# Attention through ready products of weights and memory, six weight slots, and a gate tile in two passes

## The chip, the cores and the metric

The kernel runs on one core of a Trainium2 chip. The metric is device time in microseconds (us), from the start of the program to its end; lower is better. Four compute engines work beside each other: TensorE (PE), VectorE (DVE), ScalarE (ACT) and GpSimd (POOL). SyncE (SP) issues most of the transfers, POOL and ACT issue some. The engines wait for one another by semaphores.

## The reference, cut to what matters

One layer of a hybrid decoder: 2048 prompt tokens and 8 decode tokens, model width 1024, 256 memory tokens, 4 attention heads of 256, a feed-forward width of 2816, all in fp32. The mixer before the attention (four heads of a gated short convolution and an mLSTM in chunks, then `w_out`) takes gates from a projection of 8 columns, 4 input and 4 forget gates.

```python
def mem_kv(mem, g_mem, w_xkv):
    kk, vv = jnp.split(rmsnorm(mem, g_mem) @ w_xkv, 2, axis=-1)
...
def cross_attn(xn, mk, mv, w_xq, w_xo):
    q = (xn @ w_xq).reshape(B, T, X_HEADS, X_HEAD_DIM)
    s = jnp.einsum('bthd,bmhd->bhtm', q, mk) * (X_HEAD_DIM ** -0.5)
    p = jax.nn.softmax(s, axis=-1)
    o = jnp.einsum('bhtm,bmhd->bthd', p, mv).reshape(B, T, X_HEADS * X_HEAD_DIM)
    return o @ w_xo
...
    hp = hp + mp
    hp = hp + cross_attn(rmsnorm(hp, g_cross[l]), pk, pv, w_xq[l], w_xo[l])
    hs = hs + cross_attn(rmsnorm(hs, g_cross[l]), cache_mem_k[l], cache_mem_v[l], w_xq[l], w_xo[l])
    hp = hp + swiglu(rmsnorm(hp, g_ffn[l]), w_gu[l], w_down[l])
```

The prompt attends to keys and values (`pk`, `pv`) made from 256 memory tokens; each of the 8 decode tokens has its own cached ones.

## The kernel before, in words

**Layout.** Activations stand feature-major: 8 tiles of 128 features on the partitions, tokens as columns. The prompt is cut into five blocks of 4, 3, 3, 3 and 3 chunks of 128 tokens (`BLK`). The decode tokens ride along as 8 more columns: in block `DM` for the mixer, in block `DO` for `w_out` and the queries, in block `DX` for the output projection and the feed-forward part.

**The stream of weight tiles.** All projections go through `gemm(g, ...)`. A group `g` is one tile of 128 output features: for each of 8 feature tiles three fp32r matmuls (high weights by high activations, high by low, low by high; together they stand for fp32), 24 in all, into one of three PSUM banks `gb` (L503). Groups 0 to 15 make K and V of the memory; then each block has 121 groups: the gate tile, 4 SIG tiles, 24 for the four mixer heads, 8 OUT, 8 XQ, 8 XO, then the feed-forward ones. While block 0 runs, SP loads each raw tile (512 KB, two slots `w_raw`), ACT makes its high part (`w_high`, L812), POOL its low part (L407), and SP stores the pair (1 MB) to `split_d`; blocks 1 to 4 load the pairs from there into `NS` slots `w_hl`. A slot is free when its group's matmuls are done. For groups 0 to 15 DVE makes the low parts (L1164). In the same opening loop ACT and DVE normalise block 0's input (L1153 scale, L829 high part, L1159 low part).

**Hooks.** Small matmuls are put between those of a weight tile: `hooks={k: f}` runs `f` after feature tile `k`. PE runs in program order, so a hook whose inputs are late stops the weight tiles behind it.

**Gate tile.** Its 24 matmuls give rows for input and forget gates, at partitions 32 apart. `pick_f` is one fp32 matmul in the first SIG tile that brings the forget rows to the partitions of the input rows (L550). `turn_mem` turns V in block 0 (L537).

**Attention.** The XQ tiles give the queries, which DVE and ACT split into high and low parts. `scores(h)` multiplies them with K, 256 columns a matmul (L671); `maxima` (L1422, L1425), `exps` (L1000) and `normalise` (L1431, L1433) make the softmax for one head at a time; `ptrans(h)` turns it by fp32 transposes (L681); `pv(h)` multiplies with V in plain fp32 (L688); `out_high` and `out_low` (L1012, L1438) split the result for the XO tiles. These hooks stand inside the XQ tiles for heads 0 and 1 and between parts of the first three XO tiles for heads 2 and 3. `sumsq` (L511) sums squares for the norms; `turn_row` (L561) turns gate rows into columns.

## Time and profile before

| | us |
|---|---|
| median of 3 timed runs | 2981.76 (2981.4 to 2985.2) |
| the profiled execution's own time | 2983.26 |
| its span in the trace | 2981.4 |
| PE busy | 2932.7 |
| DVE busy | 1212.0 |
| ACT busy | 762.6 |
| POOL busy | 378.2 |

The span is the time from the first to the last recorded instruction; the execution's own time has some microseconds around it. Busy times of different engines overlap. Busy PE time contains the time in which a matmul ran at a lowered clock.

### The profile page before, as it was taken

How to read it: one execution, taken by the hardware profiler on the slowest of the kernel's cores; microseconds unless marked ns; L12 is line 12 of the kernel's file. 1: busy time of each engine (PE TensorE's matmuls, PEld its weight loads, DVE VectorE, ACT ScalarE, POOL GpSimd, SP SyncE). 2: the span in 40 equal slices, each digit the busy share in tenths (PEclk: the TensorE clock that was granted, in tenths of full speed). 3: DMA queues.
4: the chain of work that ended last, by engine and by line, in shares of the span. 5: the costliest groups of instructions: out<-in, count | busy, mean ns of one | idle time of the engine just before them, and what ended most of it. 6: DMA issues, size and time to landing. Idle time of an engine off the chain costs nothing.

```text
span 2981.4 us, 39316 instructions
## 1 busy us (share of the span) xinstructions
PE 2932.7 (98%) x16212; PEld 2771.1 (93%) x16212; DVE 1212.0 (41%) x2327; ACT 762.6 (26%) x1510; POOL 378.2 (13%) x251
## 2 busy tenths in 40 slices
PE   7999999999999999999999999999999999999998
PEld 7778778888899999999999999999999999999998
DVE  6355554234624344233344546334322243442223
ACT  4433433232332220113232011322311032231001
POOL 0443434444210000000000111000000000000000
PEclk9999999999999999999999999999999999999999
DMA  5876858789776498777667989866467777647775
GB/s 198 318 261 221 281 199 302 267 283 317 283 279 245 159 328 301 267 265 282 216 227 269 339 323 370 304 225 251 170 242 260 261 258 274 227 176 250 254 268 193
DMA packets 126873, 776.11 MB, mean 260 GB/s; under 512 B 15172, under 2 KB 18692, under 8 KB 46952
## 3 DMA queue, kind: packets, MB, share of 16 engines
q1 hardware_dynamic: 109840, 710.78, 65.7%
q0 software_dynamic: 13904, 59.48, 5.9%
q10 hardware_dynamic: 2952, 3.34, 0.4%
q8 instruction: 130, 2.13, 0.3%
q14 instruction: 47, 0.39, 0.0%
HBM read 633.59 MB, written 139.95 MB: 259 GB/s over the span
## 4 chain that ended last, share of the span: by engine, by line
PE 89%; DMA 4%; DVE 2%; ACT 2%; POOL 1%; issue 1%; SPq 0%; ACTq 0%; DVEq 0%
PE gb L503 82%; DMA w_raw<-w_st 2%; PE ta L671 2%; POOL w_hl L407 1%; DMA w_hl<-split_d 1%; PE tb L688 1%; PE td L688 1%; ACT w_hl L812 1%; DMA w_raw<-w_kv 1%; PE ta L592 0%; DVE w_hl L1164 0%; PE ta L511 0%; PE tb L561 0%; PE gm L681 0%; PE tb L603 0%
## 5 line engine op out<-in xcount | busy, mean ns | idle before, releaser
L503 PE MATMUL gb<-xn_hi,w_hl 128*128 128x384 f32 (+2 forms) x6480 | 1795.7, 351 | 10.7 <-DVE xn_lo L1159 4.3
L503 PEld LDWEIGHTS gb<-xn_hi,w_hl 128*128 128x128 f32 x6480 | 1188.5, 188 | 70.8 <-DMA w_hl<-split_d 5.8
L503 PE MATMUL gb<-xn_lo,w_hl 128*128 128x384 f32 (+2 forms) x3240 | 1124.3, 347 | 0.0
L503 PE MATMUL gb<-act_hi,w_hl 128*128 128x384 f32 (+3 forms) x3296 | 874.3, 344 | 17.3 <-DVE w_hl L1164 10.7
L503 PEld LDWEIGHTS gb<-act_hi,w_hl 128*128 128x128 f32 x3296 | 599.3, 189 | 44.9 <-DVE w_hl L1164 11.0
L503 PEld LDWEIGHTS gb<-xn_lo,w_hl 128*128 128x128 f32 x3240 | 610.4, 188 | 29.0 <-issue 1.4
L503 PE MATMUL gb<-act_lo,w_hl 128*128 128x384 f32 (+3 forms) x1648 | 564.1, 342 | 0.0
L1207 DVE TENSOR_TENSOR work<-gb,r_res 128x384 f32<-128x384 f32 (+2 forms) x260 | 151.7, 585 | 633.4 <-PE gb L503 570.4
L407 POOL TENSOR_TENSOR w_hl<-w_raw,w_hl 128x1024 fp32r<-128x1024 f32 x121 | 294.6, 2439 | 484.8 <-ACT w_hl L812 484.8
L503 PEld LDWEIGHTS gb<-act_lo,w_hl 128*128 128x128 f32 x1648 | 311.9, 189 | 13.4 <-issue 0.7
L1393 DVE TENSOR_TENSOR x<-x,gb 128x384 f32<-128x384 f32 (+2 forms) x200 | 115.3, 581 | 374.6 <-PE gb L503 371.9
L812 ACT ACTIVATE w_hl<-w_raw 128x1024 fp32r<-128x1024 f32 x132 | 138.9, 1057 | 323.5 <-DMA w_raw<-w_st 160.4
L1069 ACT ACTIVATE work<-work 128x384 f32<-128x384 f32 (+2 forms) x110 | 59.9, 545 | 504.6 <-DVE work L1207 504.5
L1072 ACT ACTIVATE act_hi<-work 128x384 fp32r<-128x384 f32 (+2 forms) x110 | 60.0, 546 | 345.5 <-DVE work L1620 345.5
L986 ACT ACTIVATE work<-x 128x384 f32<-128x384 f32 (+2 forms) x120 | 65.5, 546 | 270.1 <-DVE x L1393 249.8
L1403 DVE TENSOR_TENSOR r_res<-r_res,work 128x384 f32<-128x384 f32 (+2 forms) x120 | 94.6, 788 | 69.2 <-ACT work L986 67.7
L1620 DVE TENSOR_TENSOR work<-work 128x384 f32<-128x384 f32 (+2 forms) x110 | 86.6, 787 | 30.7 <-ACT work L1069 20.5
L876 ACT ACTIVATE big<-gb,cst 128x384 f32<-128x384 f32 (+1 forms) x80 | 48.6, 608 | 197.0 <-PE gb L503 196.8
L378 POOL DMA_DIRECT2D big<-rows_d x20 | 10.9, 550 | 684.4 <-DMA rows_d<-big 684.4
L1607 DVE TENSOR_TENSOR act_lo<-work,act_hi 128x384 fp32r<-128x384 f32 (+2 forms) x110 | 85.6, 778 | 14.5 <-ACT act_hi L1072 13.9
L1303 DVE TENSOR_TENSOR work<-ta,big 128x128 f32<-128x128 f32 x64 | 18.6, 291 | 150.4 <-ACT work L957 150.4
L1406 DVE SCALAR_TENSOR_TENSOR xn_lo<-x,cst,xn_hi 128x384 fp32r<-128x384 f32 (+2 forms) x80 | 55.8, 697 | 0.0
(246 smaller groups left out, 1809.0 us busy)
## 6 DMA issues: line engine op xcount, KB each, us to landing
w_hl<-split_d SPq DMA_DIRECT2D x484, 1024.0 KB, 5.1
split_d<-w_hl SPq DMA_DIRECT2D x121, 1024.0 KB, 5.0
w_raw<-w_st SPq DMA_DIRECT2D x121, 512.0 KB, 5.9
w_raw<-w_kv SPq DMA_DIRECT2D x16, 512.0 KB, 3.4
big<-kd_d POOLq DMA_DIRECT2D x8, 1024.0 KB, 8.4
big<-vd_d POOLq DMA_DIRECT2D x8, 1024.0 KB, 11.4
x<-x_blk POOLq DMA_DIRECT2D x8, 768.0 KB, 8.9
big<-x_blk POOLq DMA_DIRECT2D x6, 768.0 KB, 6.1
```

Source lines behind the costliest of these rows:

```text
L407: pool.tensor_tensor(w_lo[:, g % NS, :], w_raw[:, g % NR, :], w_hi[:, g % NS, :].bitcast(F32), ALU.subtract).then_inc(w_lo_done, 1)
L503: mm = pe.matmul(gb[:, ps, 0:wd], a[:, s, k * P:(k + 1) * P], r[:, k, 0:wd], start=(first and k == ks[0] and i == 0), stop=(last and k == ...
L671: mm = pe.matmul(ta[:, t // 2, (t % 2) * 256:(t % 2) * 256 + 256], a[:, kt, t * P:(t + 1) * P], r[:, kt, :], start=(dt == 0 and i == 0), s ...
L812: act.activation(w_hi[:, n % NS, :], w_raw[:, n % NR, :], ACT.Copy).then_inc(w_hi_done, 1)
L986: act.activation(sq_res[:, 0:wd], x[:, e, 0:wd], ACT.Square).then_inc(res_sq, 1)
L1069: act.activation(et[:, 0:W], gt[:, 0:W], ACT.Silu).then_inc(e_ffn, 1)
L1072: act.activation(act_hi[:, f, 0:W], ht[:, 0:W], ACT.Copy).then_inc(hid_hi, 1)
L1207: return lambda ps: v.tensor_tensor(dst[:, 0:wd], ps[:, 0:wd], r_res[:, 0:wd], ALU.mult)
L1393: return lambda ps: v.tensor_tensor(x[:, e, 0:wd], x[:, e, 0:wd], ps[:, 0:wd], ALU.add)
L1403: v.tensor_tensor(acc_res[:, 0:wd], acc_res[:, 0:wd], sq_res[:, 0:wd], ALU.add).then_inc(res_acc, 1)
L1607: v.tensor_tensor(act_lo[:, f, 0:W], ht[:, 0:W], act_hi[:, f, 0:W].bitcast(F32), ALU.subtract).then_inc(hid_lo, 1)
L1620: v.tensor_tensor(ht[:, 0:W], et[:, 0:W], ut[:, 0:W], ALU.mult).then_inc(h_ffn, 1)
```

## The change

**Products.** A new phase stands between the K/V groups and block 0's gate tile. For the keys it multiplies `w_xq` of a head with that head's K, for the values that head's V with `w_xo`: 32 banks of 128x512, 12 matmuls of 256 columns each for the 16 banks of keys, 6 of 512 for the 16 of values. ACT copies the high part of a bank into one of four slots `made`, DVE subtracts the low part, and ACT issues two stores of 256 KB to where the XQ and XO pairs of `split_d` stand, in runs of 1 KB (keys) or 512 B (values). The 16 raw tiles that this takes (`w_xq` transposed, `w_xo`) come through `w_raw`, ACT and POOL ahead of block 0. Block 0 then loads its XQ and XO tiles from `split_d`, as the others do. `next_scale`, `next_high` and `next_low` for block 0 stand in this phase.

**Attention in a block.** `wide(p)` makes the scores of two heads at a time: 128 tokens stand still, the product moves, 512 columns a matmul, 24 per chunk and pair. The RMS norm comes in as a factor by token inside the softmax; `sum_cols` makes it with one-column matmuls and `norm_cols` on ACT. The turned softmax goes directly, in high and low parts (`prob_high`, `prob_low`), through XO tiles that hold V times `w_xo`. Separate scores, `pv` and `turn_mem` are gone.

**Gate tile.** Its columns 64 to 127 are the low parts of the weights (POOL copies them into the high tile), so two passes do. ACT copies the bank out, DVE adds the rows of the low columns and shifts the forget rows; the row work runs on 32 partitions (`ROWS`), and `pick_f` is gone.

**Decode tokens.** Their queries and attention outputs no longer ride along. `decode_queries` (in XO tiles 3 to 6 of block `DO`) and `decode_outputs` (in OUT tiles 3 to 6 of block `DX`) make them with 8 rows against raw weight rows, 32 fp32 matmuls of 512 columns in all, from four slots `dwt` that POOL loads in 16 transfers of 512 KB; `turn_outputs` turns the result with 8 small matmuls. More pieces of the decode attention stand at other tiles (`PIECE_AT`).

**The rest.** `NS` goes from 5 to 6. Two pairs of mixer hooks in each head are merged into one.

```diff
+G_MEM = 16
+G_KV = 32
+NPRE = 32
...
-NS = 5
+NS = 6
...
+        made = big[:, 4096:8192].rearrange("p (i s c) -> p i s c", i=4, s=2)
...
+                    pool.tensor_tensor(lo_w, raw_w, hi_w.bitcast(F32), ALU.subtract).then_inc(gate_low, 1)
+                    pool.wait_ge(gate_low, 1)
+                    lo_part, hi_part = (w.rearrange("p (k c) -> p k c", k=KT)[:, :, 64:P] for w in (lo_w, hi_w))
+                    pool.tensor_copy(hi_part, lo_part.bitcast(F32)).then_inc(w_lo_done, 1)
...
+            def decode_rows(i):
+                after(pool, dw_used, i - 3)
+                pool.dma_start(dwt[:, i % 4, :], w_dec[i] if i < KT else w_kv[G_MEM + i]).then_inc(dw_loaded[i % 4], 16)
...
+                passes = [(w_hi, hi), (w_hi, lo), (w_lo, hi)]
+                if g >= G_KV and (g - G_KV) % G_BLK == O_GATE:
+                    passes = passes[0:2]
...
+            def pre_bank(i):
+                if i < NP:
+                    read_out(pe, G_MEM - NP + i)
+                else:
+                    pe.wait_ge(pre_lo, i - NP + 1)
+                return gb[:, (G_MEM + i) % NP, :]
+            for h in range(HEADS):
+                pe.wait_ge(mem_lo, 2 * h + 2)
+                for j in range(4):
+                    i = h * 4 + j
+                    bank = pre_bank(i)
+                    for n in range(2):
+                        for dt in range(2):
+                            g = G_MEM + 2 * h + dt
+                            if j == 0 and n == 0:
+                                slot_ready(g)
+                            c = (2 * j + n) * P
+                            for f, (a, r) in enumerate([(w_hi, act_hi), (w_hi, act_lo), (w_lo, act_hi)]):
+                                mm = pe.matmul(bank[:, n * NMEM:(n + 1) * NMEM], a[:, g % NS, c:c + P], r[:, 2 * h + dt, NMEM:2 * NMEM],
+                                               start=(dt == 0 and f == 0), stop=(dt == 1 and f == 2))
+                    if j < 3:
+                        mm.then_inc(pre_done, 1)
+                    else:
+                        mm.then_inc(group_done, 2)
+            for h in range(HEADS):
...
+                for j in range(4):
+                    i = HEADS * 4 + h * 4 + j
+                    bank = pre_bank(i)
+                    mt, half = j // 2, j % 2
+                    for dt in range(2):
+                        g = G_MEM + KT + 2 * h + dt
+                        if j == 0:
+                            slot_ready(g)
+                        for f, (a, r) in enumerate([(act_hi, w_hi), (act_lo, w_hi), (act_hi, w_lo)]):
...
-                def pick_f():
-                    read_out(pe, gw(b, O_GATE))
-                    pe.matmul(td[:, 0:w_mix(b)], pick, gi[:, 0:w_mix(b)], start=True, stop=True).then_inc(f_picked, 1)
...
+                    c_hooks = {2: lambda: t_part(h, 0), 6: lambda: t_part(h, 1) or n_part(h, 0)}
                     if CH == 3:
-                        c_hooks = {2: lambda: t_part(h, 0), 4: lambda: t_part(h, 1), 7: lambda: n_part(h, 0)}
-                        h_hooks = {1: lambda: t_part(h, 2), 3: lambda: n_part(h, 1), 7: lambda: n_part(h, 2)}
...
-                def scores(h):
-                    pe.wait_ge(q_lo_done, b * 8 + 2 * h + 2)
-                    if h == 0:
-                        pe.wait_ge(r_done, r_res_at(b, 0))
-                    after(pe, exp_done, ch0(b, h))
+                def sum_cols():
+                    pe.wait_ge(res_acc, b * 27 + 9)
                     for t in range(CH):
-                        for dt in range(2):
-                            kt = 2 * h + dt
-                            for i, (a, r) in enumerate([(act_hi, mem_k_hi), (act_lo, mem_k_hi), (act_hi, mem_k_lo)]):
-                                mm = pe.matmul(ta[:, t // 2, (t % 2) * 256:(t % 2) * 256 + 256], a[:, kt, t * P:(t + 1) * P],
-                                               r[:, kt, :], start=(dt == 0 and i == 0), stop=(dt == 1 and i == 2))
-                        if t % 2 or t == CH - 1:
-                            mm.then_inc(s_done, 1)
-                def ptrans(h):
-                    pe.wait_ge(p_done, ch0(b, h) + CH)
-                    after(pe, o_lo, b * 8 + 2 * h)
-                    for mt, bank in enumerate((gm, tb)):
+                        mm = pe.matmul(td[:, t:t + 1], acc_res[:, t * P:(t + 1) * P], ones[:, 0:1], start=True, stop=True)
+                    if b == DO:
+                        mm = pe.matmul(td[0:NDEC, CHM:CHM + 1], acc_res[:, DC:DC + NDEC], ones[:, 0:1], start=True, stop=True)
+                    mm.then_inc(ssq_done, 1)
+                def score_bank(p, t):
+                    if p == 0:
+                        return gb[:, (gw(b, O_XQ) + t) % NP, :] if t < NP else gm[:, :]
+                    return (ta[:, 0, :], ta[:, 1, :], td[:, :], tb[:, :])[t]
+                def ptrans(h, mt):
+                    bank = gm if b == 0 and h < 2 else (gm, tb)[mt]
+                    pe.wait_ge(p_done, ch0(b, h // 2 * 2 + 2))
+                    pe.wait_ge(o_lo, b * 8 + 2 * h + mt - 1) if b or h == 3 else after(pe, o_lo, 2 * h + mt * (h < 2))
+                    for t in range(CH):
+                        m = pe.transpose(bank[:, t * P:(t + 1) * P], prob[:, t, h % 2, mt * P:(mt + 1) * P], ident)
+                    m.then_inc(pt_done, 1)
...
+                def wide(p, hooks):
+                    for q in range(4):
+                        g = gw(b, O_XQ) + 4 * p + q
+                        slot_ready(g)
                         for t in range(CH):
-                            m = pe.transpose(bank[:, t * P:(t + 1) * P], prob[:, t, mt * P:(mt + 1) * P], ident)
-                        m.then_inc(pt_done, 1)
-                def pv(h):
-                    pe.wait_ge(pt_evac, (b * HEADS + h) * 2 + 2)
-                    for dt, bank in enumerate((td, tb)):
-                        for mt in range(MT):
-                            mm = pe.matmul(bank[:, 0:TOK], mem_v[:, mt, h * 256 + dt * P:h * 256 + (dt + 1) * P],
-                                           prob_t[:, mt, 0:TOK], start=(mt == 0), stop=(mt == MT - 1))
-                        mm.then_inc(pv_done, 1)
-                opening(gw(b, O_XQ), W, 0)
-                q_hooks = {3: {3: lambda: scores(0)}, 4: {6: lambda: ptrans(0)}, 5: {1: lambda: scores(1), 4: lambda: pv(0)},
-                           6: {4: lambda: ptrans(1), 7: lambda: scores(2)}, 7: {3: lambda: pv(1)}}
-                for m in range(2, KT):
-                    gemm(gw(b, O_XQ + m), W, xn_hi, xn_lo, hooks=q_hooks.get(m))
+                            if q == 0 and p == 0 and t < NP:
+                                read_out(pe, gw(b, O_OUT + KT - NP) + t)
+                            if q == 0 and p == 1 and t == 2:
+                                pe.wait_ge(rcol_done, b + 1)
+                            for n in range(2):
+                                kt = 2 * q + n
+                                if p == 0 and t == 0:
+                                    pe.wait_ge(res_lo, b * 16 + kt + 1)
+                                for f, (a, r) in enumerate([(xn_hi, w_hi), (xn_lo, w_hi), (xn_hi, w_lo)]):
+                                    mm = pe.matmul(score_bank(p, t), a[:, kt, t * P:(t + 1) * P], r[:, g % NS, n * 512:n * 512 + 512],
+                                                   start=(kt == 0 and f == 0), stop=(kt == KT - 1 and f == 2))
+                            if t == CH - 1:
+                                mm.then_inc(group_done, 1)
+                            elif q == 3:
+                                mm.then_inc(s_done, 1)
+                            if (q, t) in hooks:
+                                hooks[q, t]()
+                wide(0, {(1, CH - 1): sum_cols})
+                if b == 0:
+                    wide(1, {(1, 3): lambda: ptrans(0, 0), (2, 1): lambda: ptrans(0, 1), (2, 3): lambda: ptrans(1, 0),
+                             (3, 1): lambda: ptrans(1, 1)})
+                else:
+                    wide(1, {(1, 2): lambda: ptrans(0, 0) or ptrans(0, 1), (2, 2): lambda: ptrans(1, 0) or ptrans(1, 1)})
...
                 xo(0, 0)
-                ptrans(2)
                 xo(1, 0)
-                scores(3)
                 xo(2, 0)
-                pv(2)
                 xo(0, 1)
+                ptrans(2, 0)
+                ptrans(2, 1)
                 xo(1, 1)
-                ptrans(3)
-                xo(0, 2)
-                xo(1, 2)
-                pv(3)
                 xo(2, 1)
-                xo(2, 2)
-                for i in range(3):
-                    xo(i, 3)
+                ptrans(3, 0)
+                ptrans(3, 1)
+                for h in (2, 3):
+                    for i in range(3):
...
+            def store_made(i):
+                act.wait_ge(pre_lo, i + 1)
+                h, j = (i // 4) % HEADS, i % 4
+                for s in range(2):
+                    if i < NPRE // 2:
+                        dst = split_d[O_XQ + 4 * (h // 2) + j, :, s, :].rearrange("p (n h m) -> p n h m", n=2, h=2)[:, :, h % 2, :]
+                        act.dma_start(dst, made[:, i % 4, s, :].rearrange("p (n m) -> p n m", n=2)).then_inc(pre_stored[i % 4], 16)
+                    else:
+                        kt, m0 = 2 * h + j // 2, O_XO + j % 2 * 4
+                        dst = split_d[m0:m0 + 4, :, s, kt * P:(kt + 1) * P].rearrange("m p c -> p m c")
+                        act.dma_start(dst, made[:, i % 4, s, :].rearrange("p (m c) -> p m c", m=4)).then_inc(pre_stored[i % 4], 16)
+            for i in range(NPRE):
+                pre_made(act, i)
+                after(act, pre_stored[i % 4], 32 * (i // 4))
+                act.activation(made[:, i % 4, 0, :].bitcast(F32R), gb[:, (G_MEM + i) % NP, :], ACT.Copy).then_inc(pre_hi, 1)
+                if i:
+                    store_made(i - 1)
+                if i % 4 == 3:
+                    w_high(G_MEM + i // 4 * 2)
+                    w_high(G_MEM + i // 4 * 2 + 1)
+                if i < KT:
+                    read_out(act, G_MEM - 1)
+                    act.activation(act_hi[:, i, 0:NMEM], vfeat[:, i, :], ACT.Copy).then_inc(mem_hi, 1)
...
+                def prob_high(h):
+                    for mt in range(MT):
+                        act.wait_ge(pt_done, pt0 + 2 * h + mt + 1)
+                        bank = gm if b == 0 and h < 2 else (gm, tb)[mt]
+                        act.activation(act_hi[:, 2 * h + mt, 0:TOK], bank[:, 0:TOK], ACT.Copy).then_inc(o_hi, 1)
...
+                v.wait_ge(gates_out, b + 1)
+                v.tensor_tensor(fg[:, 0:W], gb[96:96 + ROWS, g % NP, 0:W], gates[32:32 + ROWS, 0:W], ALU.add).then_inc(f_ready, 1)
+                v.tensor_tensor(gi[:, 0:W], gb[64:64 + ROWS, g % NP, 0:W], gi[:, 0:W], ALU.add).then_inc(out_v, 1)
```

## Rows read from the trace of the kernel before

**Rows 1.** The page: busy time and share of the span; chain by engine.
```profile
PE 2932.7 (98%) x16212; PEld 2771.1 (93%) x16212; DVE 1212.0 (41%) x2327; ACT 762.6 (26%) x1510; POOL 378.2 (13%) x251
PE 89%; DMA 4%; DVE 2%; ACT 2%; POOL 1%; issue 1%; SPq 0%; ACTq 0%; DVEq 0%
```

**Rows 2.** Windows: stretch, us, then busy us by engine, clock, DMA share, GB/s.
```profile
0.00:71.50 71.50, 54.22 (x388) 51.41 (x388) 47.40 (x73) 36.67 (x55) 5.39 (x6) 0.95 0.58 195
71.50:92.00 20.50, 14.34 (x42) 10.62 (x41) 14.48 (x19) 7.82 (x13) 8.74 (x5) 0.75 0.91 321
...
650.00:2981.40 2331.40, 2314.08 (x13245) 2258.18 (x13243) 891.34 (x1876) 509.55 (x1100) 139.64 (x144) 1.00 0.72 260
```

**Rows 3.** Chain of waits in block 4: start us, us, engine, tile, line, instructions.
```profile
2565.40 5.22 PE gb L503 x30
...
2618.46 2.15 PE ta L671 x18
...
2632.27 1.29 PE td L688 x4
```

**Rows 4.** Chain of waits in block 0.
```profile
92.00 0.86 PE td L550 x2
...
94.24 0.44 PE ta L537 x4
94.68 5.47 PE gb L503 x24
...
353.43 2.87 PE ta L671 x24
```

**Rows 5.** Chain of waits, gate rows turned in a later block.
```profile
2454.01 0.56 PE tb L561 x6
```

**Rows 6.** Waits of PE: who was waited for, us in total, times, longest.
```profile
PE gb L503 <- DMA w_hl<-split_d: 2.9, 6, 0.7
PE gm L681 <- DVE work L1433: 2.4, 5, 0.5
PE ta L671 <- DVE act_lo L1448: 1.7, 1, 1.7
```

**Rows 7.** DMA queues (packets, MB, share) and issues (KB each, us to landing).
```profile
q1 hardware_dynamic: 109840, 710.78, 65.7%
...
q10 hardware_dynamic: 2952, 3.34, 0.4%
...
w_raw<-w_kv SPq DMA_DIRECT2D x16, 512.0 KB, 3.4
...
big<-x_blk ACTq DMA_DIRECT2D x1, 2048.0 KB, 12.3
...
dec<-st_conv ACTq DMA_DIRECT2D x1, 32.0 KB, 1.8
```

**Rows 8.** Timeline and operations of ACT, DVE and POOL in the front.
```profile
0.76 2.21 ACTq L796 DMA_DIRECT2D x<-mem_x  x4
...
75.27 1.06 ACT L812 ACTIVATE w_hl<-w_raw 128x1024 fp32r<-128x1024 f32 x1 [4.36 <-DMA w_raw<-w_st]
...
66.13 0.69 DVE L1159 TENSOR_TENSOR xn_lo<-big,xn_hi 128x512 fp32r<-128x512 f32 x1
...
69.55 2.89 DVE L1159 TENSOR_TENSOR xn_lo<-big,xn_hi 128x512 fp32r<-128x512 f32 x1
...
76.41 2.40 POOL L407 TENSOR_TENSOR w_hl<-w_raw,w_hl 128x1024 fp32r<-128x1024 f32 x1 [4.51 <-ACT w_hl L812]
```

**Rows 9.** Groups by shape, ACT and DVE in the attention: busy, mean ns, idle before.
```profile
L1012 ACT ACTIVATE act_hi<-tb 128x512 fp32r<-128x512 f32 x4 | 2.4, 600 | 4.5 <-PE tb L688 4.5
...
L1000 ACT ACTIVATE work<-ta,work 128x256 f32<-128x256 f32 x64 | 29.6, 471 | 48.7 <-DVE work L1425 48.7
...
L1422 DVE TENSOR_REDUCE work<-ta 128x2 f32<-128x512 f32 x24 | 16.6, 690 | 24.9 <-PE ta L671 24.9
...
L1433 DVE TENSOR_SCALAR work<-work 128x256 f32<-128x256 f32 x64 | 22.6, 354 | 2.3
```

More of the change, by code:

```diff
@@ L520, in _ @@
             sumsq(acc_mix, td, NMEM)
-            for g in range(2, G_KV):
+            for g in range(2, G_MEM):
                 gemm(g, NMEM, act_hi, act_lo)
@@ L848, in _ @@
             act.wait_ge(x0_loaded, 16)
-            for g in range(G_KV):
+            for g in range(G_MEM):
                 if g < 4:
@@ L1020, in _ @@
-                rnorm(r_res, ta[:, 0, :], r_res_at(b, 0), W)
-                for m in range(2):
-                    w_high(gw(b, O_XQ + m))
-                q_high(0)
-                q_high(1)
-                q_high(2)
+                    if b == DX and e == KT - 2:
+                        act.wait_ge(dw_used, 2 * KT)
+                        for half, bank in enumerate((ta[:, 1, :], td)):
+                            act.activation(dwt[0:NDEC, 0, half * 512:half * 512 + 512], bank[0:NDEC, :], ACT.Copy).then_inc(qrow_done, 1)
@@ new lines, in _, with exps @@
+                pt0 = b * 8
+                def exps(p):
+                    after(act, pt_done, pt0 + 4 * p)
+                    for t in range(CH):
+                        act.wait_ge(mx_done, ch0(b, 2 * p) // 2 + t + 1)
+                        bank = score_bank(p, t)
+                        for i in range(2):
+                            act.activation(prob[:, t, i, :], bank[:, i * NMEM:(i + 1) * NMEM], ACT.Exp, scale=r_sc[:, t:t + 1],
+                                           bias=mx[:, t, i, 1:2], accum_out=mx[:, t, i, 2:3]).then_inc(exp_done, 1)
@@ L1176, in _ @@
             v.wait_ge(x0_loaded, 16)
-            for g in range(G_KV):
+            for g in range(G_MEM):
                 dst = mem_k if g < KT else vfeat
@@ L1472, in _ @@
+                for p in range(2):
+                    maxima(p, 0)
+                    for t in range(1, CH):
+                        maxima(p, t)
+                        normalise(p, t - 1)
+                    normalise(p, CH - 1)
+                    prob_low(2 * p)
+                    prob_low(2 * p + 1)
                 if b == DM:
@@ L1711 @@
         st += [chunk(wi, o + h * P) for s, o in enumerate(order) if s != 3]
[L1712 to L1713 removed]
+    st += [chunk(np.asarray(w_out)[0], m * P) for m in range(KT)]
+    st += [np.zeros((P, D), f) for _ in range(2 * KT)]
     gu, dn = np.asarray(w_gu)[0], np.asarray(w_down)[0]
```

528 lines of the change are left out of this document (292 added, 236 removed).

## The prediction

> **What bounds the kernel now.** I read the page's busy times first: TensorE (PE) is busy 98% of the span and holds 89% of the chain that ended last [rows 1]. The windows then say where that is not so: from 650 us on PE is busy 2314 of 2331 us at full clock, but in the first 71.5 us it is busy 54, and around the first gate tile 14 of 20.5 at a mean granted clock of 0.75, part of it at 1.2 GHz and part at 2.4 [rows 2]. So from about 92 us on, a PE microsecond taken away or added is a microsecond of the end; before that, the front of the kernel is set by loads and by ScalarE (ACT), VectorE (DVE) and GpSimd (POOL). The change does both: it removes PE work late and puts a new phase of small work at the front. The chain of waits prices each PE instruction at full rate, and I use those pieces.
>
> PE's prices: 24 fp32r matmuls 512 wide take 5.47 us, .228 each [rows 4]; 30 that are 384 wide 5.22, .174 each [rows 3]. A score stretch is 18 matmuls in 2.15 us, 24 in block 0 in 2.87, so .120 for 256 columns [rows 3, 4]. A plain fp32 matmul is two instructions: 512 wide .86 [rows 4], 384 wide .645 (1.29 for two) [rows 3], one of 4 columns .187 (0.56 for three) [rows 5].
>
> **Removed, all on PE's path.** The separate scores: 4 heads in 4 blocks of three chunks and in block 0, 16x2.15 + 4x2.87 = 45.9. The products with V in fp32: per head four of 384 or 512 columns, 16x2.58 + 4x3.44 = 55.0. Turning V (turn_mem): 4x.44 = 1.8 [rows 4]. The pick matmul: .86 + 4x.65 = 3.5. The gate tile's third pass in blocks 1 to 4: 8 matmuls x .174 x 4 = 5.6 (block 0's is in the front, below). The XQ tiles become the scores: before, 192 matmuls per block, 384 wide in three blocks, 392 in one, 512 in block 0 (33.4, 34.0 and 43.8 us); after, xn stands still and the product moves, 48 matmuls of 512 per chunk: 144x.228 = 32.8 with three chunks, 192 with four. That is .6x3 + 1.2 = 3.0 less. XO without the decode columns: 192 matmuls x 8 columns, .7. Sum 115.5.
>
> **Added to the same path.** The decode tokens' queries and outputs are now fp32 products of 8 rows against 512 moving columns: 16 tiles x 2 halves x .86 = 27.5. This is where the change pays for its saving: 8 columns riding along cost next to nothing. The small turns add 8x.19 = 1.5. sum_cols is 17 one-column fp32 matmuls, at most 17x.19 = 3.2, in place of sums that cost .86 + 4x.65 = 3.5, so -.3. Sum +28.7. Decode rows come by POOL's queue as 16 tiles of 512 KB, beside a queue that is 66% busy [rows 7]; nothing of the decode tokens' softmax is more urgent than before. The merged hooks of the mixer carry the same work; I cost them at nothing, and their cover is the weight matmuls queued on both sides (one hook that arrives late would cost what `work` now costs in such places, under 1 us each).
>
> **The new front.** Now the gate's pick matmul stands at 92.0, after 15 matmuls of the first SIG tile, so that tile would begin at 88.4 at full clock. After the change the weight phase for K and V ends about where it does now, 71 us, because its DVE work is less while one more tile comes through. Then 32 banks of products follow before the gate. For one bank PE needs 12x.120 = 1.44 us (K side) or 6x.228 = 1.37 (V side). ACT copies 512 columns out, .60 [rows 9], issues two DMAs, .55 each (four took 2.21) [rows 8], and makes a hi half of a raw tile every second bank, .53 a bank; with the K, V or xn copy of .4 to .6 on each of the first 16 banks that is 2.8 us. DVE subtracts, .69 [rows 8], and has scale and low of another tile in the first half; when POOL works beside it, such an operation took 2.89 instead of .69 [rows 8]. DMA stores 512 KB a bank in runs of 1 KB or 512 B: the small-packet queue of ACT moved 3.34 MB in 0.4% of the span, which is 280 GB/s or 1.87 us for 512 KB, and half a raw tile at q1's rate (710.78 MB in 65.7%, 363 GB/s) is .72 more [rows 7].
>
> So ACT sets the first 16 banks, 16x2.8 = 45 us. For the last 16 ACT has 1.7 + .53 = 2.2 and DMA 1.87 + .72 = 2.6, less when the raw tiles are all in; with two kept 1 MB block-0 tiles going out beside them I take 40. Start: the pairs of raw tiles must pass ACT and POOL (3.4 + 1.06 + 2.40 us for load, hi and lo) [rows 7, 8], so the chain of banks begins near 75. The gate then begins at 75 + 45 + 40 = 160, takes 16x.228 = 3.6, and some 2 us for a clock that has fallen as it had here, 0.75 [rows 2]; SIG begins at 165.6 instead of 88.4: **+77**.
>
> A page of the Trainium skill, "DMA: Bandwidth & Descriptors", section Bandwidth, says a DMA costs about 2.0 us plus its bytes at 436 GB/s and wants at least 1 MiB in one. By it a 256 KB store would take 2.6 us when alone, 5.2 for a bank whose two do not overlap; the rows agree on the fixed part only in that 512 KB land in 3.4 us [rows 7]. The same page, section Bandwidth, part "Why small descriptors are slow", speaks against runs of 256 B and not of the 512 B that are used here; no row tells the two apart.
>
> Of the waits, those of scores on q's low part (1.7) and on weight slots that arrive late (2.9) [rows 6] mostly go with the scores and the sixth slot: -4. Sum: 2983.3 + 77 - 115.5 + 28.7 - 4 = 2969.5. The profiled execution took 1.5 us more than the median run, so **2968**.
>
> **The softmax cover**, which I cost at nothing: the last chunk of the second pair goes through maximum .69, two exps .47 each, and two normalisations .35 each [rows 9], 2.3 us; with the reciprocal, the column operations and the handovers I take 3.5. Until the turns PE has 24 matmuls of XO, 24x.174 = 4.2 us (5.5 in block 0). Without that cover the chain would cost its 3.5 in five blocks, 17.
>
> **Bounds.** Front: PE alone would make it 32x1.44 = 46 us and not 85. At the other end, the 2 MB ACT load landed in 12.3 us [rows 7], 170 GB/s, 3.1 us for a bank's stores, with .72 then 3.8 a bank, 122 in all. I take 85 because ACT's own row is nearest; both ends go into the range. sum_cols: 0 to 3.2. Waits: 0 to -8. Hooks: 0 to +5. Break-even: slower by 0.2% needs the front to take 19 us longer, (85+19)/32 = 3.25 us a bank.
>
> **Rivals.**
> (a) The front keeps pace with PE, stores and copies hidden behind it: 46 instead of 85, 2929. For it: ACT's and DVE's copies alternate over three banks. Against: ACT's own work is already 2.8 a bank by its rows. Chance .07.
> (b) The other side, slower than before: the stores land slowly, so that each of the four `made` slots comes free late and ACT waits for it in order, with hi parts and DVE queued behind. At 3.8 us a bank the front is 122, +37: 3005. It decides from 3.25 us a bank. For it: 170 GB/s on ACT's load [rows 7], the small pieces of the stores, and DMA engines that are 91% busy at 321 GB/s around the gate already [rows 2]. Against: 280 GB/s for this queue's small packets. Chance .19.
> (c) The softmax takes the place of the removed waits: today PE waits for normalise five times, 2.4 us in all [rows 6]. If DVE falls one chunk (.69 + .71 [rows 9] and, as an estimate, .45 for its small column operations: 1.85) further behind, five blocks cost 9: 2978. Chance .11.
> (d) The ACT queue's stores run one after another with a fixed part each. A store of 256 KB then takes .7 of transfer and the 1.8 that 32 KB took to land here [rows 7]: 64x2.5 = 160 instead of 85, +75, 3043. This is the skill's fit told as a mechanism ("DMA: Bandwidth & Descriptors", section Bandwidth); its figure gives 64x2.6 = 166, an estimate. Against: four of ACT's loads of 256 KB were in flight together. Chance .03.
> (e) The change does not do what it says: scores as moving products would need the 101 us to come back elsewhere. PE's instruction counts exclude it; .03 is left for anything unnamed.
>
> **How the numbers follow.** Forecast .57 with its own range 2955 to 2985 (front 72 to 101 us, waits 0 to -8). 0.2% is 6 us (2975.8 to 2987.7), about what a measurement of this kernel can tell. Faster: .46 of the forecast, all of (a), .02 of (c), .02 of the rest, together .57. The same: .11 + .07 of (c) + .02 of (b) = .20. Slower: .17 of (b), .02 of (c), .03 of (d), .01 of the rest, .23. The range 2945 to 3006 leaves out (a), (d) and a tail of (b).
>
> **What would show it.** Right: SIG of block 0 begins at 160 to 170 us; PE's busy time falls by about 40 (removed 115.5, added 28.7, products 45); ACT and not DMA releases the waits between the banks; no PE wait for DVE over 1 us in the ptrans of blocks 1 to 4; a block's attention is about 20 us shorter. Wrong: waits of ACT for stores (b, d), of transposes for normalise (c), or a decode product that waits for its rows. What would make the number wrong is above all the front: each 0.3 us a bank is 10 us.

## The result: 0.4% slower

The changed kernel takes 2994.37 us (median of 7, 2992.7 to 2995.53) against 2981.76 for the kernel before on the same chip: ratio 1.004, 95% interval 1.0029 to 1.0051. The forecast was 2968, faster with .57; what came is on the side of rival (b), slower, at .19 with 3005, but by another mechanism, as the runs below show. The profiled execution has a span of 2991.6 against 2981.4, so +10.2 is what has to be explained, where the sum gave -13.8.

The page after, busy times and the chain by engine:

```profile
PE 2911.8 (97%) x15801; PEld 2721.9 (91%) x15801; DVE 1176.5 (39%) x2259; ACT 745.3 (25%) x1470; POOL 387.3 (13%) x268
PE 87%; DMA 6%; DVE 2%; ACT 2%; POOL 1%; issue 1%; ACTq 0%; SPq 0%; DVEq 0%
```

PE is 21 us less busy than in [rows 1], where the prediction counted on about 42 (115.5 removed, 28.7 and 45 added); the products alone kept PE busy for 53.0 us (25.5 at L642, 27.5 at L660) and not 45, at a mean granted clock of 0.83 in the stretch. The span is 10 us longer: PE waits 31 us more. The windows show where:

```profile
0.00:71.50 71.50, 51.22 (x348) 48.42 (x348) 40.41 (x65) 33.80 (x51) 3.45 (x6) 1.00 0.56 187
71.50:92.00 20.50, 14.64 (x96) 13.59 (x95) 16.77 (x17) 8.30 (x15) 11.08 (x5) 0.84 0.53 176
92.00:129.00 37.00, 26.46 (x159) 24.33 (x158) 27.22 (x33) 20.49 (x35) 16.40 (x7) 0.86 0.85 286
129.00:171.60 42.60, 22.92 (x78) 17.18 (x79) 12.11 (x18) 15.08 (x22) 18.36 (x9) 0.83 1.02 329
171.60:210.00 38.40, 34.12 (x140) 27.77 (x140) 8.28 (x14) 12.56 (x18) 11.90 (x5) 0.90 0.94 343
210.00:220.00 10.00, 10.00 (x30) 7.87 (x31) 1.42 (x2) 6.05 (x5) 7.00 (x6) 0.57 0.76 244
```

The columns are those of [rows 2]. Up to 92 us the DMA engines are about half busy (0.56 and 0.53) and PE waits; from 129 to 171.6 they are full (1.02) and PE is 54% busy; and the loss goes on after the gate tile, to 220 us.

The front in the timeline of ACT (start, us, operation, idle time before it and its releaser): the last high part before the banks, the first bank's copy, two pairs of store issues, and the copy of the gate tile.

```profile
83.95 1.06 ACT L980 ACTIVATE w_hl<-w_raw 128x1024 fp32r<-128x1024 f32 x1 [1.86 <-DMA w_raw<-w_kv]
84.91 0.40 ACT L1046 ACTIVATE act_hi<-x 128x256 fp32r<-128x256 f32 x1
85.22 0.58 ACT L1064 ACTIVATE big<-gb 128x512 fp32r<-128x512 f32 x1
...
100.16 0.89 ACTq L1055 DMA_DIRECT2D split_d<-big  x2
...
154.78 5.60 ACTq L1059 DMA_DIRECT2D split_d<-big  x2
...
178.38 0.69 ACT L1094 ACTIVATE big<-gb,cst 128x512 f32<-128x512 f32 x1 [0.94 <-PE gb L595]
```

The bank loop begins with the first bank's copy by ACT, at 85.2 us (forecast: near 75). The 17th comes at 128.9 and the 32nd at 170.2, so the two halves take 44 and 41 us, where 45 and 40 were forecast. The raw tiles that set the 85.2 are seen in the chain of waits:

```profile
73.08 3.68 DMA w_raw<-w_kv
76.79 1.07 ACT w_hl L980
...
77.92 2.40 POOL w_hl L472
80.33 3.59 DMA w_raw<-w_kv
83.95 1.06 ACT w_hl L980
```

A load, its high part and its low part, 7.2 us for a pair of tiles, because only two raw slots exist: the next raw tile is loaded when the low part has been made. PE does not appear there at all. In the first 16 banks the profile's chain passes twice through the landing of a store, behind which ACT gets a free `made` slot. This is the mechanism of rival (b); it is there, but small beside the 85 us of the banks:

```profile
100.56 4.10 DMA split_d<-big
...
112.10 4.00 DMA split_d<-big
```

PE itself waits in the banks for the low part by DVE (25.9 us in all, at L660 and L642), which follows ACT's copy. The prediction had named ACT as the releaser.

The late part of the kernel is as costed. Block 1's attention in the chain (start, us, tile):

```profile
1047.79 0.56 PE td L803 x6
1048.35 8.31 PE gb L839 x36
1056.66 2.72 PE ta L839 x12
...
1074.33 4.19 PE gb L595 x24
1078.51 0.33 PE gm L821 x3
1078.84 0.33 PE tb L821 x3
1079.17 2.10 PE gb L595 x12
```

Wide scores take .227 to .231 a matmul, sum_cols .56 for three, and the 24 XO matmuls (4.19) hide the softmax, the one wait for it being .8 us in block 0: no wait stands between them and the turns at L821. From block 0's second sum of squares to block 1's the trace has 601.7 us instead of 623.2, 21.5 less.

### The profile page after: what moved, and what is told of

Read it like the earlier page. It is cut to its first block, busy times and chain, and to the rows that moved or that the text cites. A ratio compares the mean times of both kernels' runs of the same rounds, so it can differ in the third digit from the quotient of the medians.

```text
span 2991.6 us, 38477 instructions
## 1 busy us (share of the span) xinstructions
PE 2911.8 (97%) x15801; PEld 2721.9 (91%) x15801; DVE 1176.5 (39%) x2259; ACT 745.3 (25%) x1470; POOL 387.3 (13%) x268
## 4 chain that ended last, share of the span: by engine, by line
PE 87%; DMA 6%; DVE 2%; ACT 2%; POOL 1%; issue 1%; ACTq 0%; SPq 0%; DVEq 0%
PE gb L595 76%; PE gb L839 3%; DMA w_raw<-w_st 2%; PE ta L839 2%; DMA w_raw<-w_kv 2%; POOL w_hl L472 1%; PE td L839 1%; ACT w_hl L980 1%; DMA big<-kd_d 1%; DMA w_hl<-split_d 1%; PE ta L708 0%; PE tb L683 0%; DVE work L1515 0%; DMA split_d<-big 0%; PE gm L821 0%
## 5 line engine op out<-in xcount | busy, mean ns | idle before, releaser
L595 PE MATMUL gb<-xn_hi,w_hl 128*128 128x384 f32 (+2 forms) x5800 | 1588.4, 350 | 6.5 <-issue 4.3
L595 PEld LDWEIGHTS gb<-xn_hi,w_hl 128*128 128x128 f32 x5800 | 1063.0, 188 | 56.0 <-issue 8.1
L595 PE MATMUL gb<-xn_lo,w_hl 128*128 128x384 f32 (+2 forms) x2920 | 1014.0, 347 | 0.0
L595 PEld LDWEIGHTS gb<-xn_lo,w_hl 128*128 128x128 f32 x2920 | 550.3, 188 | 24.6 <-issue 0.5
L1413 DVE TENSOR_TENSOR work<-gb,r_res 128x384 f32<-128x384 f32 (+2 forms) x220 | 128.2, 585 | 549.2 <-PE gb L595 512.3
L1616 DVE TENSOR_TENSOR r_res<-r_res,work 128x384 f32<-128x384 f32 (+2 forms) x120 | 81.4, 679 | 56.5 <-ACT work L1198 54.9
L839 PE MATMUL gb<-w_hl,xn_hi 128*128 128x512 f32 x240 | 77.6, 397 | 0.0
```

Of the source, the lines that this page charges most:

```text
L595: mm = pe.matmul(gb[:, ps, 0:wd], a[:, s, k * P:(k + 1) * P], r[:, k, 0:wd], start=(first and k == ks[0] and i == 0), stop=(last and k == ...
L839: mm = pe.matmul(score_bank(p, t), a[:, kt, t * P:(t + 1) * P], r[:, g % NS, n * 512:n * 512 + 512], start=(kt == 0 and f == 0), stop=(kt ...
L1413: return lambda ps: v.tensor_tensor(dst[:, 0:wd], ps[:, 0:wd], r_res[:, 0:wd], ALU.mult)
L1616: v.tensor_tensor(acc_res[:, 0:wd], acc_res[:, 0:wd], sq_res[:, 0:wd], ALU.add).then_inc(res_acc, 1)
```

## The experiments

Each kernel ran beside the kernel before on the same chip; its median there was 2980.4 to 2981.8 in all. Five times were read from each trace: the first, 17th and 32nd bank copy, the copy of the gate tile, and the second sum of squares of block 0, by which block 0's attention is over.

Each trace is of one execution. e3 and e8 leave out a part of the work and have one run each.

| run | 1st | 17th | 32nd | gate copy | sum | time | ratio (95%) |
|---|---|---|---|---|---|---|---|
| before | | | | 86.5 | 448.3 | 2981.8 | |
| changed | 85.2 | 128.9 | 170.2 | 178.4 | 514.5 | 2994.4 | 1.004 (1.0029 to 1.0051) |
| e1 | 80.2 | 123.7 | 166.3 | 174.3 | 503.6 | 2986.2 | 1.0018 (1.0009 to 1.0027) |
| e2 | 86.4 | 126.5 | 164.6 | 174.8 | 513.5 | 2990.8 | 1.0034 (1.0022 to 1.0047) |
| e3 | 85.3 | 126.4 | 167.2 | 175.9 | 508.2 | 2985.9, one run | |
| e4 | 83.6 | 126.6 | 172.4 | 180.1 | 516.8 | 2992.6 | 1.0043 (1.0028 to 1.0058) |
| e5 | 70.7 | 114.2 | 156.1 | 164.9 | 485.9 | 2967.9 | 0.9954 (0.9939 to 0.9969) |
| e6 | 70.8 | 114.8 | 158.4 | 166.7 | 488.3 | 2969.3 | 0.9958 (0.9941 to 0.9974) |
| e7 | 71.5 | 112.6 | 147.9 | 155.5 | 481.8 | 2963.4 | 0.9940 (0.9925 to 0.9955) |
| e8 | 87.1 | 130.5 | 170.4 | 180.1 | 517.6 | 2982.2, one run | |
| e9 | 70.7 | 110.1 | 144.9 | 151.7 | 473.7 | 2956.4 | 0.9923 (0.9906 to 0.9939) |
| e10 | 70.4 | 111.1 | 146.2 | 153.9 | 475.9 | 2958.0 | 0.9925 (0.9910 to 0.9939) |
| e11 | | | | 80.3 | 432.0 | 2982.4 | 1.0007 (0.9998 to 1.0016) |
| e12 | 83.6 | 127.2 | 170.5 | 177.6 | 513.1 | 2991.4 | 1.0035 (1.0023 to 1.0048) |

### Five slots (e1) and the sixth one later (e12)

```diff
-NS = 6
+NS = 5
```

> The changed kernel with five weight slots. Theory 'the front is late because ACT looks six tiles ahead': ACT enters the bank loop after the high part of one raw tile less, so the first bank copy comes at about 81 us, not 85, and the gate tile begins 3 to 4 us earlier than 171.6; the reload waits of blocks 1 to 4 (2.9 us before) come back; together 2990 to 2995. Rival 'six slots carry the later blocks': the front is unchanged and the waits for split pairs grow past 5 us, over 2998.

The front came as the first theory had it, 5.0 us earlier at the first copy and 4.1 at the gate tile, and the total went lower still, by 8 us (6.7 between the profiled spans). Two things add up. The first is at the very start: in the changed kernel ACT waits in the opening loop for the raw tile of the sixth slot, which lands 7.49 us after it was asked for, with the 2 MB load of x under way, where the tile before took 3.75:

```profile
20.20 0.49 ACT L1023 ACTIVATE act_hi<-x,cst 128x256 fp32r<-128x256 f32 x1
25.50 1.06 ACT L1026 ACTIVATE w_hl<-w_raw 128x1024 fp32r<-128x1024 f32 x1 [4.80 <-DMA w_raw<-w_kv]
```

The first two sums of squares come at 31.3 and 48.3 us with six slots, at 26.7 and 43.3 with five and at 26.0 and 42.5 before. The second is in block 0. Waits of PE from 165 to 460 us with six slots, then with five:

```profile
...
PE gb L595 <- issue: 4.3, 1, 4.3
PE tb L683 <- ACT big L1117: 4.3, 1, 4.3
PE tb L719 <- DVE work L1515: 4.2, 4, 1.2
```

```profile
PE gb L595 <- issue: 6.3, 1, 6.3
PE tb L719 <- DVE work L1515: 5.3, 4, 2.0
...
PE tb L683 <- ACT big L1117: 0.7, 1, 0.7
```

ACT makes the gate rows behind the high parts of tiles six ahead, and those tiles are late; the turn of the rows waits 4.3 us for them with six slots and 0.7 with five. Other waits take part of this back: the wait by `issue` stands before the gate copy, and from that copy to the second sum PE is idle 9.3 us of 336.1 with six slots and 7.0 of 329.3 with five. So 2.3 of the 6.8 us are waiting and 4.5 are busy time. After the long wait in the changed kernel the granted clock is 0.57 for ten us (the window 210 to 220 above, in part at 1.2 GHz), after PE had been busy 5.7 of 10 us; in the same place e1 has 1.00. At 0.57, ten us lose 4.3, nearly all of the 4.5. Against that, from block 0's second sum to the last, six slots take 2466.1 us and five 2470.3: the sixth slot does give back 4 us in the later blocks (with five slots PE waits 3.9 us in all for pairs that are loaded again, with six not at all), and costs 11 up to there.

e12 separates the two. Six slots, the sixth tile's parts made after the normalisation of the memory that the opening loop begins with (ACT's side of the edit; DVE's is the same):

```diff
-                if k < NS:
+                if k < NS - 1:
                     act.wait_ge(w_loaded[k % NR], 16 * (k // NR) + 16)
...
             for g in range(G_MEM):
                 if g < 4:
                     next_sq(0, 2 * g)
+                if g == 0:
+                    act.wait_ge(w_loaded[(NS - 1) % NR], 16 * ((NS - 1) // NR) + 16)
+                    act.activation(w_hi[:, NS - 1, :], w_raw[:, (NS - 1) % NR, :], ACT.Copy).then_inc(w_hi_done, 1)
...
```

> The changed kernel with its six weight slots, but the high and low part of the sixth tile made after the opening normalisation instead of within it. Theory 'the sixth slot costs 5 us at the very start, since ACT and DVE wait in the opening loop for a raw tile that comes behind the 2 MB load of x': the first two sums of squares come at about 26 and 43 us as before (31.3 and 48.3 now), the bank loop still starts late, at 82 to 85 us, since ACT must pass the high part of tile 21 first; total 2989 to 2993. Rival 'the 5 us are made good by the wait for tile 21 anyway': first bank copy at 85, total 2993 to 2996. Rival 'five slots gain because fewer tiles are looked ahead in the bank loop and block 0': the turned gate rows still wait for ACT 4 us.

The first sum is at 27.2 again, but of its 4 us only 1.6 are left at the first bank copy and 0.8 at the gate: the high part of tile 21 has to pass in any case. The other 3.4 us between e12 and e1 (83.6 and 80.2) are one tile of the chain, half of the 7.2. The turned rows still wait 3.6 us. So the opening wait by itself costs little; looking one tile further ahead costs both times, before the banks and in block 0. The total is 2991.4; its interval (1.0023 to 1.0048) overlaps that of the changed kernel (1.0029 to 1.0051), so no gain in time is shown.

### Who sets the banks' pace (e2, e3, e4)

e2 takes ACT's 64 issues away (`store_made` goes to SyncE's queue, four banks at a time between the raw loads).

> The changed kernel with the 64 stores of the product phase issued by SyncE in place of ACT. Theory 'ACT's own work sets the first 16 banks': they fall from 44 us to about 30, the gate tile begins at 155 to 162 instead of 171.6, total 2980 to 2988. Rival 'the phase is bound by bytes that the DMA engines move': the first 16 banks are shorter, the last 16 take as much longer, the gate tile begins at 168 or later, total 2991 or more.

Neither theory: the first half took 40 us, not 30. ACT's issues were 3.5 us of its 43.6; the chain of waits of this run goes through ACT's high parts and then DVE:

```profile
94.01 1.05 ACT w_hl L996
95.06 0.31 ACT act_hi L1073
...
95.40 1.50 DVE act_lo L1397
96.89 2.75 DVE big L1352
99.64 0.61 DVE big L1393
```

Beside a POOL subtraction (POOL is busy from 94.2 to 99.1) DVE takes 2.75 us for the scaling that takes .74 alone in the same loop, and the bank's low part stands behind it. The second half took 38.

e3 stores a bank as one transfer of 512 KB in runs of 4 KB. It leaves out the order in which the attention reads the products, so its result is not the layer's:

```diff
-                for s in range(2):
-                    if i < NPRE // 2:
...
+                act.dma_start(split_d[O_XQ + i // 2][:, i % 2, :], made[:, i % 4, :, :].rearrange("p s c -> p (s c)")).then_inc(pre_stored[i % 4], 16)
```

> The changed kernel with one store of 512 KB for each bank in runs of 4 KB, to a wrong place within the XQ and XO pairs, so the attention reads products in a scrambled layout. Theory 'bytes, not small runs, bind the last 16 banks': these still take 36 us or more (41 now), the first 16 gain the second issue, .47 each, 44 to about 37. Rival 'the runs of 512 B are slow': the last 16 banks fall to 30 us or less.

The last half took 40.8 us: eight times longer runs do not shorten it, so the 512 B runs are not what holds it. They are not free either: the share of the DMA engines there fell from 1.02 to 0.91, at 343 GB/s instead of 325. With a share of 0.91 the engines are not quite full, and what holds the pace of this run was not isolated. The first half gained 2.5 us and not 7. The whole run was 8 us shorter than the changed kernel, 2.5 of it by the gate copy and 3.8 in block 0; it is one run, and which of the three things that it changes (half as many issues, longer runs, other places) does this is open.

e4 gives the product tiles' low parts to DVE (`w_low` in place of POOL's subtraction for groups 16 to 31).

> The changed kernel with the low parts of the 16 product tiles made by DVE (1.23 us) instead of POOL (2.40 us, and DVE slowed beside it). Theory 'the chain load, high, low of raw tiles sets the entry into the bank loop': a pair of tiles takes 6.0 us instead of 7.2, first bank copy at 81 us instead of 85, gate tile 3 to 6 us earlier, total 2988 to 2991. Rival 'DVE has no room in the phase': banks wait for DVE, gate tile not earlier than 171, total 2994 or more.

The first copy came 1.6 us earlier (forecast 4), but the last half took 46 us, and the gate copy came 1.7 us later than in the changed kernel. By itself it is no gain.

### Four raw slots (e5) and what they open (e6, e7, e9, e10)

The memory of the sixth pair slot holds two more raw tiles:

```diff
-NS = 6
+NS = 5
...
-NR = 2
+NR = 4
```

> The changed kernel with five weight slots and four raw slots (the sixth pair slot's memory holds two more raw tiles). Theory 'the front runs at the pace of raw tiles that share two slots': the K/V groups end some 8 us earlier than the 70 us of before, the first bank copy comes at 66 to 72 us (80.2 with two raw slots), the gate tile begins 10 to 20 us earlier than 167.6 (e1), total 2966 to 2977. Rival 'the DMA engines are the bound from the start, by bytes': the gate tile begins within 4 us of e1's and the total stays at 2982 to 2988.

2967.9 us, almost the number that was forecast for the changed kernel, but that is chance: the front is not as forecast here either, and this is another kernel. Both halves keep their length (43.5 and 42); they start 9.5 us earlier than in e1, and block 0 from the gate copy to its second sum takes 321.0 us instead of 329.3 (336.1 with six slots, 361.8 before). The windows of e5:

```profile
0.00:70.00 70.00, 53.68 (x396) 51.77 (x397) 48.26 (x71) 37.41 (x57) 9.80 (x8) 0.98 0.68 226
70.00:114.00 44.00, 32.30 (x204) 29.55 (x202) 34.14 (x42) 24.03 (x42) 18.47 (x9) 0.88 0.83 272
114.00:156.00 42.00, 21.46 (x78) 15.57 (x78) 11.59 (x16) 14.64 (x22) 18.79 (x9) 0.84 1.04 344
```

The DMA engines move 226 GB/s in the first 70 us instead of 187: they start on the bytes sooner. Only the last stretch is full. The edit does two things, four raw slots and one pair slot less; e1 has the second alone, so the comparison with e1 shows what the raw slots do. In block 0, PE's waits of over 4 us are gone; one of 0.8 is left.

e6 also changes ACT's order in the opening:

```diff
+                if g >= KT:
+                    read_out(act, g - KT)
+                    act.activation(act_hi[:, g - KT, NMEM:2 * NMEM], mem_k[:, g - KT, :], ACT.Copy).then_inc(mem_hi, 1)
+                if g < G_MEM - 1:
+                    w_high(g)
...
```

> As the run with five pair slots and four raw slots, and in the opening loop ACT copies K's high part before it waits for a raw tile, and leaves the last raw tile's high part until after the second bank. Theory 'order on ACT holds the banks back': the first bank copy comes 3 to 6 us earlier than with four raw slots alone, the gate tile 2 to 5 us earlier. Rival 'with four raw slots ACT never waits there': both within 1 us.

The rival was right: nothing moved. Once raw tiles are ready ACT has nothing to be reordered around.

e7 adds SyncE's stores (the edit of e2).

> As the run before, with the 64 stores issued by SyncE. Theory 'with raw tiles ready ACT's own 2.8 us a bank is the bound of the first 16 banks': 44 us become 30 to 36, total 3 to 8 us below the run before. Rival 'DMA is the bound by then': no change within 2 us, as the last 16 banks take longer.

6 us less than e6, but not where it was expected: the first half went from 44.0 to 41.1, the second from 43.5 to 35.4. One reading of the second half would be that ACT was held up before: in the changed kernel a pair of issues on ACT took up to 5.6 us (timeline above) while the DMA engines were full, and the next bank's copy stood behind it. The windows of the second half, e6 and then e7, say something else:

```profile
114.80:158.40 43.60, 23.50 (x78) 17.31 (x78) 11.69 (x16) 14.56 (x23) 18.61 (x9) 0.81 1.04 343
```

```profile
112.60:148.00 35.40, 24.71 (x84) 18.14 (x83) 12.15 (x16) 14.69 (x22) 16.02 (x8) 0.84 1.09 346
```

The rate is the same. It is the bytes that differ, 14.9 MB in e6 and 12.3 in e7, and 2.7 MB at 345 GB/s are 7.7 of the 8.1 us. In e6 the two 1 MB stores of the output K and V are issued within this stretch; in e7 they are issued at 148.9 and 150.8, behind it, and the stores of the last four banks after them. Part of it is only put off: from the gate copy to block 0's second sum e7 takes 326.3 us and e6 321.6. What ACT's long issues cost by themselves is not shown.

e10 is e7 with these two 1 MB stores moved to before the banks:

```diff
-                if off == 6:
-                    read_out(sp, G_MEM - 1)
+                if g == 12:
+                    read_out(sp, KT - 1)
                     sp.dma_start(o_mk.rearrange("p (k m) -> p k m", k=KT), mem_k).then_inc(kv_stored, 16)
+                if g == 19:
+                    read_out(sp, G_MEM - 1)
                     sp.dma_start(o_mv, vfeat.rearrange("p k m -> p (k m)")).then_inc(kv_stored, 16)
```

> As the run with four raw slots, ACT's order and stores by SyncE, with only the two 1 MB stores of the output K and V moved ahead of the bank loop. Theory 'they take DMA time where it is short': the gate tile's copy comes 0 to 5 us earlier than 155.5 and block 0's first waits shrink, total 2958 to 2962. Rival 'the bytes are the same, moved only': within 1 us of 2963.4.

5.4 us less, most of it in block 0 (322.0 us from gate copy to sum, 326.3 in e7). The two ran on different chips; against the kernel before beside them the difference is 4.6 us, and the intervals of the ratios still overlap. The traces speak against the rival "moved only": the 4.3 us in block 0 that e7 had lost come back, and the first bank copy is not later (70.4 against 71.5), so here bytes moved to where the DMA engines are not full cost next to nothing. e9 is e10 with the low parts on DVE:

> As the run with four raw slots, ACT's order and stores by SyncE (2963.4), with the product tiles' low parts made by DVE and the stores of the output K and V issued before the bank loop. Theory 'DVE slowed beside POOL sets the first 16 banks': four banks take 9 us or less (10.3 now), the gate tile's copy comes at 146 to 152 us instead of 155.5, total 2955 to 2961. Rival 'DVE has no room for 1.23 us more': four banks take over 10 us, total 2962 or more.

With raw tiles ready the same edit that did nothing in e4 shortens the first half by 1.3 us and the gate copy comes 2.1 earlier, one execution against one; four banks of it still take 9.3 to 10.8. The total, 2956.4, is the lowest of the study, .9923 of the kernel before, but its difference to e10 (1.6) is inside their spread.

### The decode products (e8) and the kernel before with four raw slots (e11)

```diff
-                        mm = pe.matmul(bank[half][0:NDEC, :], lhs, dwt[:, i % 4, half * 512:half * 512 + 512],
+                        mm = pe.matmul(bank[half][0:NDEC, 0:8], lhs, dwt[:, i % 4, half * 512:half * 512 + 8],
```

> The changed kernel with the 32 fp32 products of the decode tokens 8 columns wide instead of 512, so 504 of 512 columns of their queries and outputs are left out. Theory 'each costs PE .86 us and is not hidden': XO of block DO and OUT of block DX are shorter by about 32 x (.86 - .19) = 21 us, total 2973. Rival 'their cost is the wait for rows loaded by POOL's queue': less than 10 us are saved, and PE waits for the rows stay.

The time was 2982.2 (one run) with a span 11.5 us shorter, between the two. In the changed kernel each product costs what was forecast (`ta` and `td`, two tiles in an XO tile):

```profile
1608.46 0.95 PE ta L867 x2
1609.41 0.86 PE td L867 x2
```

With narrow products the loads of the rows come out from under them; waits of PE from 1500 to 2400 us in e8 (in the changed kernel PE waits for no row there):

```profile
PE ta L867 <- DMA dwt<-w_dec: 3.7, 2, 3.0
PE ta L773 <- DMA dwt<-w_kv: 3.1, 1, 3.1
```

So both were partly right: 21 us of PE time could go, but 6.8 of them would be waits for rows. The front of this run was 1.5 to 3 us later as well, as runs of one kernel can differ.

```diff
-NS = 5
+NS = 4
...
-NR = 2
+NR = 4
```

> The kernel before with four weight slots and four raw slots in the same memory. Theory 'the raw tile chain held its K/V groups too': the opening shortens by 4 to 8 us, the blocks lose 0 to 4 us to waits for pairs, total 2974 to 2981. Rival 'four pair slots are too few': over 2984.

The kernel before gains in the same place: its gate copy comes 6.2 us earlier and block 0's second sum 16.3 us earlier. But with four pair slots PE waits for reloads in the later blocks,

```profile
PE gb L503 <- DMA w_hl<-split_d: 10.5, 11, 3.2
```

where it waits 2.9 us in all in [rows 6], and the end is unchanged, between theory and rival. These waits are about half of the 14 us that blocks 1 to 4 lose; the rest was not traced.

## Why the prediction was wrong

By the same points as in the sum, in us of the profiled spans (after minus before):

| stretch | forecast | measured |
|---|---|---|
| up to SIG of block 0 | +77 | +90.0 |
| block 0 from there to its second sum | -29.6 | -23.8 |
| blocks 1 to 4 | -61.2 | -56.0 |
| together | -13.8 | +10.2 |

For the kernel before, the first row takes the 88.4 us of the prediction as the start of SIG.

**The step that failed** is the start of the bank loop, "so the chain of banks begins near 75". The prediction had the terms of the chain of raw tiles (3.4 for the load, 1.06 for the high part, 2.40 for the low part: 6.9 us, and 7.2 were measured for two tiles), but 75 is only 4 us behind the 71 at which it let the K and V groups end, less than one pass. ACT has to make the high parts of six tiles ahead, three pairs, before the first copy, and the first of them was ready at 66: 66 + 2 x 7.2 + 3.6 is 84. 85.2 was measured. "One more tile comes through" in the opening was costed at nothing, and takes 4.8 us of waiting at its place, though e12 shows that 1.6 of it are left at the first copy. The late start is 10 of the 13 us by which the front was too short in the sum; the gate tile and the banks are the rest. The runs bear this out: one tile less moved the first copy by 3.4 us (e12 and e1), raw tiles that are ready moved it by 9.5 more (e5), and the total followed both times.

**The banks themselves** were sized right, 44 and 41 for 45 and 40, but the reason given for the first half was wrong in part. "So ACT sets the first 16 banks": e2 took the issues off ACT, 1.1 us of its 2.8 a bank, 18 in all, and got 3.5 of 44 us. With raw tiles ready and stores elsewhere it is 39 to 41 us still, with DVE's work in it. For the second half the sentence on bytes is borne out by e6 and e7, where the time follows the bytes at one rate; in the changed kernel the DMA engines' share there is 1.02. The fit of the Trainium skill that rival (d) tells as a mechanism ("DMA: Bandwidth & Descriptors") stands in that page's section "Anatomy of one DMA — SWDGE (gpsimd) path" and is for transfers that GpSimd issues, which these were not. As a price for each store it is not borne out here: 64 stores of 256 KB landed in a median of 4.0 us but overlapped, 2.7 us a bank. Nor did rival (b) take place at its price: the banks took 2.7 us each and not 3.25, with 8 us of landings of stores in the chain.

**The gate tile** took 6.75 us for its 16 matmuls, not 3.6 + 2: nearly all of it ran at 1.2 GHz (.42 a matmul), after a stretch with PE half busy.

**Block 0** was costed as if the front ended at the gate tile. It does not: the DMA engines are 94% busy until 210 us, the raw tiles come late, and ACT, in order, holds the gate rows. From the gate copy to the second sum PE is idle 9.3 us; it was 8.0 before, and the sum took 1.7 from that. So 3 of the 5.8 us that are missing here are waits, and 4.3 are the lowered clock (10 us at 0.57), for which the sum had no term; some 1.5 went the other way and are not traced. What stands queued behind ACT was asked in rival (b) for the banks only.

**Blocks 1 to 4** came within 5 us of 61. From one block's second sum to the next, block 1 gave 21.5 and block 4 21.3, where 21.6 was counted: scores, V products, pick and third pass are priced right by the rows of before. The rest of the forecast and of the miss lies in blocks 2 and 3, where the decode products stand. Of the missing 5 us, 1.5 are a fall of the clock in block 3 (below) and .7 the first products of the eight decode hooks, .95 instead of .86. About 3 us are not traced further.

**The softmax cover** held, rival (c) is out: the waits of turns for the softmax are 0.8 us in all (2.4 in [rows 6]). **Decode**: 32 x .86 was right, but for the first product of each hook. **The sixth slot** was worth what it was costed at, about 4 us in the later blocks (e1), but with it ACT looks further ahead, and that was costed at nothing.

## What to carry to other kernels

A pipeline stage in an in-order engine that looks N tiles ahead delays whatever stands behind it by N tiles' worth of the slowest chain, so more slots can make a phase that is short of loads slower: count how many passes of the chain the first useful instruction has to wait for, not one. Where a new phase is put ahead of a bandwidth-bound one, look at the DMA share of the stretches before it; here the same memory cost 8 us as a sixth pair slot (changed kernel against e1) and gained 18 as two more raw slots (e5 against e1), which let loads run in an idle stretch. Follow a backlog past the end of the phase that makes it. And when a stretch gets shorter, compare the bytes that were moved in it before calling it faster: in e7 most of the gain of the second half was traffic that came later.

## What the hardware did that I had not expected

Eight small fp32 matmuls in a row (`turn_outputs`, 8 columns each, 1.88 us) were followed by a fall to 1.2 GHz although PE was never idle. Chain, then windows of that place:

```profile
2106.44 1.88 PE tb L780 x16
2108.32 1.24 PE gb L595 x6
2109.55 9.82 PE gb L839 x36
...
2119.94 8.31 PE gb L839 x36
```

```profile
2105.00:2110.00 5.00, 5.00 (x34) 4.60 (x32) 1.09 (x3) 0.99 (x3) 0.00 (x0) 0.97 0.46 190
2110.00:2114.00 4.00, 4.00 (x13) 3.13 (x12) 1.40 (x4) 1.03 (x2) 0.00 (x0) 0.61 0.80 262
2114.00:2118.00 4.00, 4.00 (x19) 3.31 (x18) 0.00 (x0) 0.00 (x0) 0.00 (x0) 1.00 0.38 109
```

The 36 matmuls after it took 9.82 us instead of 8.31. In e5 the same place ran at 1.00, so it does not come every time; that the small matmuls cause it was only seen, not tested. And an issue of two transfers on ACT took .89 us with the DMA engines at 0.85 and up to 5.6 us with them full, with the engine's next copy behind it.
